# Gate and up weights of an expert: two 2 MB transfers with two releases, or one 4 MB transfer with one

## The reference, cut to what matters

```python
def expert_block(args):
    xb, e = args
    return (jax.nn.silu(xb @ w_gate[e]) * (xb @ w_up[e])) @ w_down[e]
...
'w_expert_gate': nrm(ks[20], (L, N_EXPERTS, D_MODEL, D_EXPERT), ...)   # 32 x 1024 x 512
'w_expert_up':   nrm(ks[21], (L, N_EXPERTS, D_MODEL, D_EXPERT), ...)   # 32 x 1024 x 512
'w_expert_down': nrm(ks[22], (L, N_EXPERTS, D_EXPERT, D_MODEL), ...)   # 32 x 512 x 1024
```

## Time and profile before

| | before |
|---|---|
| median of 3 runs | 1119.75 us (1119.45 to 1121.8) |
| the profiled execution, its own time | 1121.75 us |
| span of its profile | 1119.8 us |
| PE busy | 977.3 us (87%) |
| DVE, ACT, POOL busy | 24%, 15%, 8% |
| HBM read | 247.95 MB |

### The profile page before, as it was taken

One profiled execution on the slowest core, in us unless ns is written; L12 is line 12 of the kernel. 1 busy time (PEld: TensorE's weight loads), 2 busy tenths in 40 slices (PEclk: granted clock), 3 DMA queues, 4 the chain that ended last, 5 costly groups with the idle time before them and its releaser, 6 DMA issues.

```text
span 1119.8 us, 11234 instructions
## 1 busy us (share of the span) xinstructions
PE 977.3 (87%) x4489; PEld 560.8 (50%) x4489; DVE 270.2 (24%) x608; ACT 166.3 (15%) x459; POOL 87.8 (8%) x97
## 2 busy tenths in 40 slices
PE   4999899988999999999995999878779788878885
PEld 4644666556888888885454334323223223323321
DVE  4565534681000000000234411110110110110110
ACT  3222343442000000000110111100000000000110
POOL 2000000000000000000001112201011011011101
PEclk8999899997999999999995999999998998899898
DMA  7430201021733333305536899999999999999992
GB/s 272 114 95 13 76 1 38 1 58 28 223 76 76 76 75 75 75 0 234 235 135 270 341 388 391 399 396 410 399 398 404 404 398 408 406 398 412 405 407 59
DMA packets 69708, 253.80 MB, mean 227 GB/s; under 512 B 9049, under 2 KB 50009, under 8 KB 57360
## 3 DMA queue, kind: packets, MB, share of 16 engines
q1 hardware_dynamic: 63591, 240.42, 56.5%
q0 software_dynamic: 6080, 12.89, 4.3%
HBM read 247.95 MB, written 14.58 MB: 234 GB/s over the span
## 4 chain that ended last, share of the span: by engine, by line
PE 57%; DMA 33%; DVE 6%; issue 2%; ACT 1%; SPq 0%; POOL 0%; POOLq 0%; DVEq 0%; ACTq 0%
DMA arena<-in_w_gu 32%; PE ps L1390 21%; PE ps L1500 8%; PE ps L1236 7%; PE ps L1418 5%; PE ps L1265 4%; PE ps L1519 3%; PE ps L1294 2%; DMA x<-in_x 1%; DVE arena L902 1%; PE ps L1279 1%; PE ps L1303 1%; PE ps L1335 1%; PE ps L1437 1%; PE ps L1490 1%
## 5 line engine op out<-in xcount | busy, mean ns | idle before, releaser
L1500 PE MATMUL ps<-arena 128*64 128x512 f32 x512 | 236.1, 611 | 17.2 <-DMA arena<-in_w_gu 17.1
L1501 PE MATMUL ps<-arena 128*64 128x512 f32 x512 | 236.1, 611 | 0.0
L1390 PE MATMUL ps<-arena 128*128 128x272 f32 x1024 | 234.9, 392 | 1.0 <-ACT arena L668 1.0
L1390 PEld LDWEIGHTS ps<-arena 128*128 128x128 f32 x1024 | 194.5, 190 | 41.4 <-ACT arena L668 1.4
L1519 PE MATMUL ps<-arena,x 128*64 128x512 f32 x512 | 137.6, 686 | 60.8 <-issue 49.9
L1500 PEld LDWEIGHTS ps<-arena 128*64 128x64 f32 x512 | 67.7, 139 | 156.5 <-issue 123.9
L1519 PEld LDWEIGHTS ps<-arena,x 128*64 128x64 f32 x512 | 45.2, 156 | 150.5 <-issue 149.5
L592 ACT ACTIVATE arena<-ps 64x512 f32<-64x512 f32 (+7 forms) x127 | 53.8, 445 | 271.8 <-PE ps L1519 182.1
L1089 DVE SCALAR_TENSOR_TENSOR x<-ps,list_w,x 64x512 f32<-64x512 f32 x32 | 23.8, 743 | 285.3 <-ACT x L738 285.3
L555 POOL DMA_INDIRECT out_y<-arena,list_i x32 | 45.6, 1426 | 410.0 <-PE ps L1490 285.6
L1236 PE MATMUL ps<-arena 128*128 128x512 f32 (+2 forms) x208 | 77.4, 529 | 0.0
(11 more groups left out here) (200 smaller groups left out, 692.3 us busy)
## 6 DMA issues: line engine op xcount, KB each, us to landing
arena<-in_w_gu SPq DMA_DIRECT2D x64, 2048.0 KB, 44.6
arena<-in_w_ed SPq DMA_DIRECT2D x32, 2048.0 KB, 43.5
arena<-in_w_in SPq DMA_DIRECT2D x16, 512.0 KB, 4.7
arena<-in_w_in SPq DMA_DIRECT2D x5, 1024.0 KB, 9.0
arena<-in_w_in SPq DMA_DIRECT2D x2, 2048.0 KB, 7.8
arena<-in_w_attn SPq DMA_DIRECT2D x16, 256.0 KB, 6.4
arena<-in_w_pool SPq DMA_DIRECT2D x8, 512.0 KB, 7.4
arena<-in_w_out SPq DMA_DIRECT2D x2, 2048.0 KB, 14.5
```

What stands on the lines that cost most here:

```text
L1390: ins = mm(ps[:, 4 * h + j, 0:HALF], w[:, j, k, :], src[:, k, h * HALF:(h + 1) * HALF], start=k == 0, stop=k == KD - 1)
L1500: mm(ps[0:C, 2 + s, :], xT[s][:, j, :], w[:, jj, 0, :], start=j == 0, stop=j == JX - 1)
L1501: ins = mm(ps[64:64 + C, 2 + s, :], xT[s][:, j, :], w[:, jj, 1, :], start=j == 0, stop=j == JX - 1)
```

## The change

The host lays up and gate of an expert together without the halves: 32 KB contiguous per partition, 4 MB per expert. One transfer fetches them, into one area, with one semaphore; `gate_up` waits once, does its 8 pairs, and releases once; SP refills on `gu_ready` alone. The semaphores `ga_used`, `ga_full` and `gb_full` are gone. The area in SBUF, the matmuls, their order and the bytes are the same.

```diff
-        w_gu = [[area(at + 4096 * h, JX // 2, 2, DE) for h in range(2)] for at in RING]
+        w_gu = [area(at, JX, 2, DE) for at in RING]
...
             def load_gu(e, s):
-                sp.dma_start(w_gu[s][0], a["w_gu"][expert_at(e), 0]).then_inc(ga_full[s], 16)
-                sp.dma_start(w_gu[s][1], a["w_gu"][expert_at(e), 1]).then_inc(gb_full[s], 16)
+                sp.dma_start(w_gu[s], a["w_gu"][expert_at(e)]).then_inc(gu_full[s], 16)
...
             for e in range(NSLOT, NE):
-                sp.wait_ge(ga_used, e - NSLOT + 1)
-                sp.dma_start(w_gu[e % NSLOT][0], a["w_gu"][expert_at(e), 0]).then_inc(ga_full[e % NSLOT], 16)
                 sp.wait_ge(gu_ready, e - NSLOT + 1)
-                sp.dma_start(w_gu[e % NSLOT][1], a["w_gu"][expert_at(e), 1]).then_inc(gb_full[e % NSLOT], 16)
+                load_gu(e, e % NSLOT)
                 if e > NSLOT:
                     sp.wait_ge(dn_ready, e - NSLOT)
                     load_down(e - 1, (e - 1) % NSLOT)
...
             def gate_up(e, s, ring, full):
 
                 pe.wait_ge(xe_taken, e + 1)
-                for h, (landed, used) in enumerate(((ga_full, ga_used), (gb_full, gu_ready))):
-                    pe.wait_ge(landed[ring], full)
-                    for jj in range(JX // 2):
-                        j, w = h * (JX // 2) + jj, w_gu[ring][h]
-                        mm(ps[0:C, 2 + s, :], xT[s][:, j, :], w[:, jj, 0, :], start=j == 0, stop=j == JX - 1)
-                        ins = mm(ps[64:64 + C, 2 + s, :], xT[s][:, j, :], w[:, jj, 1, :], start=j == 0, stop=j == JX - 1)
-                    ins.then_inc(used, 1)
+                pe.wait_ge(gu_full[ring], full)
+                for j in range(JX):
+                    mm(ps[0:C, 2 + s, :], xT[s][:, j, :], w_gu[ring][:, j, 0, :], start=j == 0, stop=j == JX - 1)
+                    ins = mm(ps[64:64 + C, 2 + s, :], xT[s][:, j, :], w_gu[ring][:, j, 1, :], start=j == 0, stop=j == JX - 1)
+                ins.then_inc(gu_ready, 1)
...
-        "w_gu": np.stack([f(w_expert_up)[0].reshape(NE, P, 2, JX // 2, DE), f(w_expert_gate)[0].reshape(NE, P, 2, JX // 2, DE)],
-                         axis=4).transpose(0, 2, 1, 3, 4, 5),
+        "w_gu": np.stack([f(w_expert_up)[0].reshape(NE, P, JX, DE), f(w_expert_gate)[0].reshape(NE, P, JX, DE)], axis=3),
```

More of the change, by code:

```diff
@@ L321, in build @@
         item_ready = sem("item_ready")
-        ga_full = [sem(f"ga_full{s}") for s in range(NSLOT)]
-        gb_full = [sem(f"gb_full{s}") for s in range(NSLOT)]
+        gu_full = [sem(f"gu_full{s}") for s in range(NSLOT)]
         dn_full = [sem(f"dn_full{s}") for s in range(NSLOT)]
@@ L328, in build @@
         xe_taken = sem("xe_taken")
-        ga_used = sem("ga_used")
         gu_ready = sem("gu_ready")
@@ L504, in _ @@
                     expert = sp.value_load(item_i[0:1, bass.ds(i, 1)], min_val=0, max_val=NE - 1)
-                    for h, full in ((0, ga_full), (1, gb_full)):
-                        sp.dma_start(w_gu[0][h], a["w_gu"][bass.ds(expert, 1), h].squeeze(0)).then_inc(full[0], 16)
+                    sp.dma_start(w_gu[0], a["w_gu"][bass.ds(expert, 1)].squeeze(0)).then_inc(gu_full[0], 16)
                     sp.dma_start(w_down[0], a["w_ed"][bass.ds(expert, 1)].squeeze(0)).then_inc(dn_full[0], 16)
```

## The result

The changed kernel takes 1131.18 us (median of 5 runs, 1127.14 to 1132.16) against 1119.75 us: a ratio of 1.0089 with a 95% interval from 1.0069 to 1.0109, so about 10 us slower (the medians alone are 11.4 us apart). Slower was forecast, but by 4.0 us, and the time lies above the range.

The account below looks back on a forecast made before the run. The prediction took the DMA stream of weights to bound the experts' part. Its terms, 3.4 - 1.5 + 1.6 + 0.5 = +4.0 us on the median of 1119.75, gave 1123.8 us, range 1117 to 1127.5 (its own terms' ends 1122.2 to 1126.5).

Parts of the forecast that it names:

- What bounds the kernel: Experts' part: the DMA stream of weights sets the pace from about 720 us, 16.74 us per expert against PE's 11.95.
- Term 1: Start of the refills: without the early half releases the continuous stream starts later, and nothing gives it back, +3.4 us.
- Terms 3 and 4: Last expert: all 16 matmul rows follow the last landing, +1.6 us; PE's clock may be low after the wait, +0.5.
- Term 2: Stream of weights: 8 fewer pieces per engine and expert, and one completion less, save time, -1.5 us (0 to -2.6).
- Hidden and unchanged: Side effects in the experts' part, gathers sharing engines with pieces of twice the size among them, taken to cost nothing.
- The rival that came nearest: Stream beside gathers and adds: fewer pieces give back 0.4 us per expert, 11.6 us in all, so 1113.7 us; 11%.
- The rival of a fixed cost per transfer: Weight transfers: a cost paid in a row, 3.4 us each by the rows, is saved 29 times, giving 1025 us; 1%.

Follow-up runs that it names:

- one_release: The kernel before, with both 2 MB transfers of gate and up issued on the one release `gu_ready`, still two waits on PE: 1123.8 us, 1.0024.
- one_transfer_16k: The changed kernel, its 4 MB transfer taking each partition as two pieces of 16 KB from the HBM layout of before: 1125.98 us, 1.0055 to the kernel before.
- layout_only: The kernel before, with its two transfers and two releases, reading from the changed kernel's HBM layout: 1120.32 us, 1.0000.
- one_release_one_wait: As one_release, and PE waits for both halves before the first matmul: 1126.27 us, 1.0051 to the kernel before.

## Why the prediction was wrong

The direction was right, and the size was off by 6 us. By its own steps:

- **What bounds the kernel: right.** The stream sets the pace from about 700 us on; PE waits once per expert (the view of waits from 720 to 1110 us has 23 waits for gate and up, 74.0 us in all, the longest 5.1) and PE's work never became the bound. With less for the stream to carry (no rows) the kernel was 60 us faster.
- **Term 1, the late start: right.** +3.4 forecast, +2.7 measured by one_release [+1.0, +4.5]. In the profiled execution of the changed kernel the engines did not run dry a second time (share 1.00 at 630 us): PE's step of the second expert took 10.6 us instead of 12.3, with a higher clock, so the refill came sooner than I had placed it. That isn't owed to the change: the step took 12.3 us in one_transfer_16k, and 10.6 in layout_only, which has the waits and releases of before. The windows that show the clock, the kernel before (624 to 630 us, PEclk 0.72) and the changed one (622 to 628 us, 1.00):

```profile
624.00:630.00 6.00, 5.95 (x22) 2.30 (x24) 5.38 (x18) 0.38 (x1) 0.00 (x0) 0.72 0.97 377
```

```profile
622.00:628.00 6.00, 5.88 (x30) 2.42 (x32) 5.38 (x18) 0.38 (x1) 0.00 (x0) 1.00 1.09 434
```

- **Terms 3 and 4, the end and the clock: 2.1 forecast, 3.1 in the trace, 3.0 by the step from one_release to one_release_one_wait.** The end was right; the clock took about 1.5 us, not 0.5. I had reckoned a wait of 2 to 3.5 us ahead of the last `gate_up`, and it was 4.13: with one wait per expert PE stands at the landing of each gate and up, so all of its slack lies in front of it. The Trainium skill, "TensorE: Matmul & The Clock Gate", section "HAM oscillation", warns of a wait for the next slice of weights that puts the clock down. The trace agrees (rows of 1.06 us instead of 0.59 behind the wait), and it cost time at the one place where PE is on the path.
- **Term 2, the pace of the stream: the step that failed.** It said -1.5 us (0 to -2.6); what the runs show in its place is about +4 us (from one_transfer_16k to the changed kernel, 0.0034), or +5 by the trace (7.6 us late at its end less 2.6 at its start). Its own content, fewer pieces cost less, was right and rather too small: without rows the larger pieces gave back 3 us by the trace. What failed is the sentence that stands under "Hidden and unchanged", which put the price of the shared engines at nothing: that the gathers share them with pieces of twice the size, and that it costs only if they land too late for PE. They landed in time (14.5 us against 20.4 that were free, no wait of PE for them), and the price was paid on the other side, by the stream, whose pieces grew longer beside the gathers by 0.54 us per expert before and 0.90 after. Over 29 experts that is some 10 us lost against some 4 gained, an estimate from the two traces.
- **What is shown of the cause and what isn't.** Shown: not the release, not the wait, not the layout, not the 4 MB transfer, and not the size of the pieces by itself, since without row traffic it costs nothing. It is the size together with the row traffic. The gathers are what does it: 8.2 us against 2.0, and the weight pieces lengthened beside gathers and not beside adds. It doesn't need uneven engines (11 us when rotated). Open: why a weight piece takes longer beside a gathered row, and why longer pieces lose more. These runs have no kernel that changes the gathers' own form.
- **The rival that came nearest** was the one on the other side: a stream that flows worse or better beside the rows. I had named the gap between 402 and 433 GB/s, and asked only whether larger pieces would close it. It closed nothing, and opened by 6 GB/s.
- The rival of a fixed cost per transfer, paid in a row, had 1%: one 4 MB transfer for two of 2 MB made no difference beyond the noise of 2 to 3 us (1.0055 against 1.0051). In this kernel's full queue no such cost is seen.

## What to carry to other kernels

Merging transfers saved nothing here, where the queue behind them is deep, and it moves both ends of the stream: the first refill waits for a whole slot, and after the last landing a whole slot's work is left, at a low clock if the engine had to wait for it. Where a stream of large pieces shares the DMA engines with gathered rows, price the change from both sides: the rows may be in time and the stream may pay. And ask which engine serves which row: the fullest one seems to pace the stream, and shifting the first place by expert was worth more (-0.45%) than any size of piece tried.

## What the runs showed of the hardware that I had not expected

- An indirect transfer of 64 rows deals them out one by one, place c to engine c mod 16, and skipped rows are not made up for. The profile doesn't number the engines; this is the assignment that fits three kernels. With the rows at every fourth place, 16 and then the next 16, two groups of four engines carried nearly all of them (by the count 128 to 112 rows each, the others 31 or fewer), and the kernel was 1.74% slower; rotated it was 0.45% faster. By the experts' counts of rows in these inputs 47 rows more on the fullest engine cost 19.5 us, 0.41 us for a row gathered and added.
- A gather lengthens the weight pieces beside it (16 KB: 0.713 us near a gathered row, 0.617 elsewhere); an add doesn't (mean 0.612 with adds only, 0.616 without rows), and costs 0.327 us for a row of 4 KB, where a gathered row takes 0.159 us at the least.
- A gather of some 34 rows of 4 KB lands later the larger the pieces of the stream beside it are: in 6.8, 8.1, 10.7 and 14.5 us beside pieces of 4, 8, 16 and (for gate and up) 32 KB.
- From 16 KB on larger pieces bring almost nothing in this stream: 428 GB/s at 16 KB and 430 with two thirds at 32 KB, without rows.
